# Cross-attention's value products in groups of 512 columns, each over both halves of the features

## What is computed

```python
def _cross_attention(h, mem_n, w_q, w_kv, w_o):
    B, S, _ = h.shape
    M = mem_n.shape[1]
    q = (h @ w_q).reshape(B, S, XA_HEADS, XA_HEAD_DIM)
    kv = (mem_n @ w_kv).reshape(B, M, 2, XA_HEADS, XA_HEAD_DIM)
    s = jnp.einsum('bshd,bmhd->bhsm', q, kv[:, :, 0]).astype(jnp.float32) * XA_HEAD_DIM ** -0.5
    p = jax.nn.softmax(s, axis=-1)
    o = jnp.einsum('bhsm,bmhd->bshd', p.astype(kv.dtype), kv[:, :, 1]).reshape(B, S, XA_HEADS * XA_HEAD_DIM)
    return o @ w_o
```

## Time and profile before

| | |
|---|---|
| Median of three runs | 1274.87 us (1273.26 to 1274.92) |
| The profiled execution, time | 1273.56 us |
| The profiled execution, span of the trace | 1271.6 us |
| TensorE (PE) busy | 1254.7 us, 99% of the span |
| Weight loads (PEld) busy | 1064.4 us, 84% |
| VectorE (DVE) busy | 823.1 us, 65% |
| ScalarE (ACT) busy | 666.0 us, 52% |
| GpSimd (POOL) busy | 208.7 us, 16% |

### The profile page before, as it was taken

One profiled execution on the slowest core, in us unless ns is written; L12 is line 12 of the kernel. 1 busy time (PEld: TensorE's weight loads), 2 busy tenths in 40 slices (PEclk: granted clock), 3 DMA queues, 4 the chain that ended last, 5 costly groups with the idle time before them and its releaser, 6 DMA issues.

```text
span 1271.6 us, 18501 instructions
## 1 busy us (share of the span) xinstructions
PE 1254.7 (99%) x6756; PEld 1064.4 (84%) x6756; DVE 823.1 (65%) x1185; ACT 666.0 (52%) x1119; POOL 208.7 (16%) x247
## 2 busy tenths in 40 slices
PE   8999999999999999999999999999999999999998
PEld 6888888899988888888888888888999798888886
DVE  5657777785566575555576568777857566755554
ACT  6454447664546464444564544565746465544442
POOL 1725541000001010000055246300000100100000
PEclk9999999999999999999999999999999999999999
DMA  9755453424525355555455554544255243655551
GB/s 346 270 188 179 168 194 146 166 100 170 196 100 182 106 229 198 198 183 182 167 185 192 198 198 165 192 156 160 74 182 204 112 150 133 235 191 177 181 181 62
DMA packets 32441, 222.34 MB, mean 175 GB/s; under 512 B 3584, under 2 KB 4096, under 8 KB 6784
## 3 DMA queue, kind: packets, MB, share of 16 engines
q1 hardware_dynamic: 30080, 209.28, 45.7%
q10 hardware_dynamic: 2304, 12.29, 2.6%
HBM read 219.46 MB, written 2.10 MB: 174 GB/s over the span
## 4 chain that ended last, share of the span: by engine, by line
PE 97%; DVE 1%; ACT 1%; issue 1%; DMA 0%; SPq 0%; POOLq 0%; ACTq 0%; POOL 0%; DVEq 0%
PE PS L1682 91%; PE PS L1769 2%; PE PS L1795 1%; PE PS L1991 1%; DVE w_lo L1161 1%; DMA raw<-in_weights 0%; ACT x_hi L717 0%; DVE x_lo L1164 0%; PE PS L1975 0%; PE PS L2273 0%; PE PS L2035 0%; PE PS L1922 0%; DVE h L1164 0%; PE PS L2042 0%; DVE work L1164 0%
## 5 line engine op out<-in xcount | busy, mean ns | idle before, releaser
L1161 DVE TENSOR_TENSOR w_lo<-raw,w_hi 128x1024 fp32r<-128x1024 f32 (+1 forms) x378 | 482.4, 1320 | 220.5 <-ACT w_hi L676 216.5
L676 ACT ACTIVATE w_hi<-raw 128x1024 fp32r<-128x1024 f32 x368 | 369.0, 1054 | 231.0 <-PE PS L1682 226.7
L1682 PE MATMUL PS<-w_hi,x_hi 128*128 128x512 f32 (+2 forms) x1136 | 438.3, 386 | 5.9 <-DVE x_lo L1164 3.0
L1682 PE MATMUL PS<-w_lo,x_hi 128*128 128x512 f32 (+2 forms) x1136 | 426.1, 375 | 0.0
L1682 PE MATMUL PS<-w_hi,x_lo 128*128 128x512 f32 (+2 forms) x1136 | 420.5, 376 | 0.0
L1682 PEld LDWEIGHTS PS<-w_hi,x_hi 128*128 128x128 f32 x1136 | 214.4, 189 | 48.9 <-issue 7.2
L1682 PEld LDWEIGHTS PS<-w_hi,x_lo 128*128 128x128 f32 x1136 | 214.3, 189 | 39.6
L1682 PEld LDWEIGHTS PS<-w_lo,x_hi 128*128 128x128 f32 x1136 | 214.8, 189 | 35.6 <-issue 0.5
L1682 PE MATMUL PS<-w_hi,hid_hi 128*128 128x512 f32 x336 | 131.5, 391 | 0.0
L1682 PE MATMUL PS<-w_lo,hid_hi 128*128 128x512 f32 x336 | 130.8, 389 | 0.0
L730 ACT ACTIVATE work<-PS,st 128x256 f32<-128x256 f32 x88 | 42.0, 478 | 155.5 <-PE PS L1682 153.9
(11 more groups left out here) (277 smaller groups left out, 1306.4 us busy)
## 6 DMA issues: line engine op xcount, KB each, us to landing
raw<-in_weights SPq DMA_DIRECT2D x194, 1024.0 KB, 4.7
pmat<-in_mats ACTq DMA_DIRECT2D x3, 1568.0 KB, 8.4
gain<-in_post ACTq DMA_DIRECT2D x8, 512.0 KB, 3.7
zone<-mem_scratch ACTq DMA_DIRECT2D x2, 1024.0 KB, 6.5
raw<-in_weights SPq DMA_DIRECT2D x3, 512.0 KB, 7.9
h<-in_x SPq DMA_DIRECT2D x2, 512.0 KB, 6.3
zone<-in_mem SPq DMA_DIRECT2D x1, 1024.0 KB, 9.7
mem_scratch<-zone ACTq DMA_DIRECT2D x1, 1024.0 KB, 5.6
```

Source lines behind the costliest of these rows:

```text
L676: a.activation(w_hi[s][:, c_], raw[s][:, c_], ACT.Copy).then_inc(sem[hi_done[s]], 1)
L1161: return v.tensor_tensor(o, x_, y_, op)
L1682: return t_.matmul(o, a_, b_, start=first, stop=last)
```

## The change

Per layer, the four value units become two pairs of units, (14, 15) and (16, 18). Each pair holds 512 value columns: its first unit carries the upper four feature tiles of them and its second unit the lower four. `values_half(pair, t, half)` is one part: four feature tiles, 12 matmuls of 512 columns, for token tile t. The two halves of one t accumulate into all of bank 1, which ScalarE then copies with `evac_values`. The semaphore `proj_half` tells of the end of t = 0 (so its count per layer goes from 5 to 7), `unit_done` that of t = 1. The host lays the weights out accordingly. There are still eight parts, but their order over the units is 14, 15, 14, 15, 16, 18, 16, 18 where it was 14, 14, 15, 15, 16, 16, 18, 18.

Because units 16 and 19 have one slot and one `unit_done`, `phi_unit(3)` (unit 19) moves behind part 7, which is the last use of unit 16; `times_values(1)` moves ahead of both, and the fold of the block rows behind part 8. VectorE's copy of the block rows moves behind `attention_out(1)`. On ScalarE the last evacuation moves from behind the tanh of the block rows to ahead of it, behind the split of unit 22.

```diff
-                proj_done=11, proj_half=5, s5_us=1, s5_u_dve=1, s5_t=1, s5_lb_act=1, s5_lb_dve=1, s5_k=1, s5_kd=1,
+                proj_done=11, proj_half=7, s5_us=1, s5_u_dve=1, s5_t=1, s5_lb_act=1, s5_lb_dve=1, s5_k=1, s5_kd=1,
...
+                def evac_values(pair, t):
+                    if t == 0:
+                        act.wait_ge(*E.at("proj_half", 5 + pair))
                     else:
-                        i = a.activation(xv[:, :, (q - 4) * UC:(q - 3) * UC],
-                                         v3(bank(KV_BANK[q]), "p (t n) -> p t n", t=TT), ACT.Copy)
-                    i.then_inc(sem["xkv_done"], 1)
+                        s, n, _ = mid(l, KV_UNITS[5 + 2 * pair])
+                        act.wait_ge(*E.at(unit_done[s], n + 1))
+                    act.wait_ge(*E.at("x_split", FILL[FI_MEM] + KT))
+                    a.activation(xv[:, t, pair * 512:(pair + 1) * 512], bank(1), ACT.Copy).then_inc(sem["xkv_done"], 1)
...
                 split_mid(22)
+                evac_values(1, 1)
                 act.wait_ge(*E.at("phi_x", 1))
                 a.activation(v3(hx2, "p (a n) -> p a n", n=NC_CMP), v3(hx2, "p (a n) -> p a n", n=NC_CMP),
                                  ACT.Tanh, scale=GELU_S).then_inc(sem["phi_th"], 1)
-                evac_kv(7)
                 split_mid(21)
...
                 split_mid(18)
                 attention_copy(1)
-                s, n, _ = mid(l, PHI_UNITS[3])
-                dve.wait_ge(*E.at(unit_done[s], n + 1))
-                v.tensor_copy(phi_rows, bank(0)).then_inc(sem["phi_h"], 1)
...
                 attention_out(1)
+                s, n, _ = mid(l, PHI_UNITS[3])
+                dve.wait_ge(*E.at(unit_done[s], n + 1))
+                v.tensor_copy(phi_rows, bank(0)).then_inc(sem["phi_h"], 1)
...
+                def values_half(pair, t, half):
+                    s, _, ns = mid(l, KV_UNITS[4 + 2 * pair + half])
+                    if half == 0:
+                        pe.wait_ge(*E.at("xkv_done", 4 + 2 * pair + t))
+                    pe.wait_ge(*E.at(split_done[s], ns + 1))
+                    for k in range(KT // 2):
+                        c_ = slice(k * 2 * UC, (k + 1) * 2 * UC)
+                        i = three([(x_tile(half * KT // 2 + k, t), (w_hi[s][:, c_], w_lo[s][:, c_]))], bank(1),
+                                  half == 0 and k == 0, half == 1 and k == KT // 2 - 1)
+                    if t == 1:
+                        i.then_inc(sem[unit_done[s]], 1)
+                    elif half == 1:
+                        i.then_inc(sem["proj_half"], 1)
...
-                kv_half(4, 0)
+                values_half(0, 0, 0)
                 probs_transposed(3)
-                kv_half(4, 1)
+                values_half(0, 0, 1)
                 times_values(3)
...
                 probs_transposed(1)
-                kv_half(6, 1)
-                phi_unit(3)
-                pe.wait_ge(*E.at("xkv_done", 7))
-                kv_half(7, 0)
+                values_half(1, 0, 1)
                 pe.wait_ge(*E.at("nsa_v", 1))
                 times_values(1)
+                values_half(1, 1, 0)
+                phi_unit(3)
+                values_half(1, 1, 1)
                 pe.wait_ge(*E.at("phi_h", 1))
...
                 i.then_inc(sem["phi_t"], 1)
-                kv_half(7, 1)
                 pe.wait_ge(*E.at("att_out", 3))
                 scores(2)
```

More of the change, by code:

```diff
@@ L943, in attention_t, with evac_keys @@
                     a.activation(probs_t[:, 0:1024], bank(5, 2), ACT.Copy).then_inc(sem["att_tc_act"], 1)
[L945 removed]
+                def evac_keys(q):
                     s, n, _ = mid(l, KV_UNITS[q])
                     act.wait_ge(*E.at(unit_done[s], n + 1))
[L948 to L955 removed]
+                    a.activation(zone[:, q * 512:(q + 1) * 512], bank(KV_BANK[q]), ACT.Copy).then_inc(sem["xkv_done"], 1)
+                def evac_values(pair, t):
+                    if t == 0:
+                        act.wait_ge(*E.at("proj_half", 5 + pair))
+                    else:
+                        s, n, _ = mid(l, KV_UNITS[5 + 2 * pair])
+                        act.wait_ge(*E.at(unit_done[s], n + 1))
+                    act.wait_ge(*E.at("x_split", FILL[FI_MEM] + KT))
+                    a.activation(xv[:, t, pair * 512:(pair + 1) * 512], bank(1), ACT.Copy).then_inc(sem["xkv_done"], 1)
                 def group_squares(groups, name, ready):
@@ L1003, in _ @@
                 split_mid(10)
-                evac_kv(0)
+                evac_keys(0)
                 attention_t(0)
-                evac_kv(1)
+                evac_keys(1)
                 split_mid(12)
@@ L1013, in _ @@
                 i.then_inc(sem["fox_nc"], 1)
-                evac_kv(2)
+                evac_keys(2)
                 act.wait_ge(*E.at("fox_tq", 1))
@@ L1017, in _ @@
                 split_mid(14)
-                evac_kv(3)
+                evac_keys(3)
                 attention(3)
@@ L1022, in _ @@
                 attention_t(3)
-                evac_kv(4)
+                evac_values(0, 0)
                 split_mid(16)
@@ L1026, in _ @@
                 a.activation(nsa_q[0:HD, :], bank(6, 2)[0:HD], ACT.Copy).then_inc(sem["nsa_tc_act"], 1)
-                evac_kv(5)
+                evac_values(0, 1)
                 attention(1)
@@ L1031, in _ @@
                 attention_t(1)
-                evac_kv(6)
+                evac_values(1, 0)
                 group_squares((0, 2), "att_out", 2)
@@ L1087, in xq_rows @@
                     if t == 0:
-                        act.wait_ge(*E.at("proj_half", 5))
+                        act.wait_ge(*E.at("proj_half", 7))
                     else:
@@ L2020, in kv_half @@
                             pe.wait_ge(*E.at("x_split", FILL[FI_MEM] + k + 1))
-                        if q < 4:
-                            c_ = slice(k * UC + part * P, k * UC + (part + 1) * P)
-                            i = three([((w_hi[s][:, c_], w_lo[s][:, c_]), (xh3[:, k], xl3[:, k]))],
-                                      o[:, part * S:(part + 1) * S], k == 0, k == KT - 1)
-                        else:
-                            c_ = slice(k * UC, (k + 1) * UC)
-                            i = three([(x_tile(k, part), (w_hi[s][:, c_], w_lo[s][:, c_]))],
-                                      o[:, part * UC:(part + 1) * UC], k == 0, k == KT - 1)
+                        c_ = slice(k * UC + part * P, k * UC + (part + 1) * P)
+                        i = three([((w_hi[s][:, c_], w_lo[s][:, c_]), (xh3[:, k], xl3[:, k]))],
+                                  o[:, part * S:(part + 1) * S], k == 0, k == KT - 1)
                     if part == 1:
                         i.then_inc(sem[unit_done[s]], 1)
+                def values_half(pair, t, half):
[11 more added lines that the diff above has]
+                        i.then_inc(sem["proj_half"], 1)
                 def fox_heads(at, b, name):
@@ L2150, in _ @@
                 i.then_inc(sem["nsa_t"], 1)
-                pe.wait_ge(*E.at("xkv_done", 5))
-                kv_half(5, 0)
+                values_half(0, 1, 0)
                 pe.wait_ge(*E.at("att_out", 2))
@@ L2383, in kv @@
         def kv(q):
-            put(tall(g["xa_w_kv"][l][:, q * UC:(q + 1) * UC]))
+            if q < 4:
+                put(tall(g["xa_w_kv"][l][:, q * UC:(q + 1) * UC]))
+            else:
+                at_, half = q // 2 * 2 * UC, q % 2
+                u = g["xa_w_kv"][l][:, at_:at_ + 2 * UC].reshape(KT, P, 2 * UC).transpose(1, 0, 2)
+                put(u[:, half * KT // 2:(half + 1) * KT // 2].reshape(P, UNIT))
         def phi(q):
```

11 lines of the change are left out of this document (2 added, 9 removed).

## The result

The changed kernel takes **1289.02 us** (median of 4 runs, 1288.55 to 1289.58) against 1274.07 for the kernel before: ratio 1.0117, 95% interval 1.0103 to 1.0132. It is 1.2% slower. The forecast was 1286.4 (1282.5 to 1290.0). The profiled execution has a span of 1286.7 us against 1271.6: 15.1 more, where 12.1 were forecast.

The account below looks back on a forecast made before the run. TensorE bounds the kernel (97% of the chain). Per layer, waits of 7.2 us less 1.1 saved; two layers +12.1 us, giving 1285.7 from the profile or 1287.0 from the median; the middle, 1286.4 us, range 1282.5 to 1290.

Parts of the forecast that it names:

- A: Before part 2, TensorE waits for VectorE's low half of unit 15: 2.0 us per layer.
- B: Before part 6, TensorE waits for VectorE's low half of unit 18: 1.5 us per layer.
- C: At the fold of the block rows, TensorE waits for VectorE's copy of them: 0.2 us per layer.
- D: Before the block's hidden product, TensorE waits for hidden rows, behind ScalarE's tanh and unit 22's split: 1.2 us per layer.
- E: Before out_rows(1, 0), TensorE waits for VectorE, late after splits of units 22 and 21: 2.3 us per layer.
- Savings: Eight value parts with 512-column matmuls, each 0.14 us shorter: 1.1 us less per layer.
- rival 4: The clock falls to the 1.2 GHz level at one wait of each layer: 2.0 us per layer, 1290.4 us; 6%.
- Rival 1: The tail is hidden (C to E don't occur), leaving A and B less savings: 4.8 us, 1279.7 us; 8%.
- Rivals 2 and 3: 2: early-wanted units are ready, only savings remain, 1272.7 us, 4%; 3: matmuls and waits cancel, about 1.3 more, 2%.

Follow-up runs that it names:

- e1_form: Kernel before, own order, each value part as 12 matmuls of 512 columns, not 24 of 256, lower four feature tiles left out; 1271.85 us, ratio 0.9987.
- e3_units: Changed kernel with unit 19 back behind part 6 (own semaphore), copy and fold where they were, tanh ahead of last evacuation; 1278.25 us, ratio 1.0036.
- e2_tail: e1_form with the change's places of unit 19, the fold, VectorE's copy and ScalarE's last evacuation, value units in old order; 1280.47 us, ratio 1.0051.
- e5_order: Changed kernel; ScalarE splits unit 21 before the tanh, unit 22 after; VectorE splits unit 22 behind mixer_lo and compressed scores; 1280.90 us, ratio 1.0068.
- e10_mixorder: e4_cover with units 14 and 15 in old form and order, and unit 21 split before unit 22 on ScalarE and VectorE; 1273.03 us, ratio 0.9995.
- e9_fill2: e7_fill plus three more 512-column matmuls, written to bank 5, between scores(2) and the wait for phi_hid; 1289.96 us, ratio 1.0126.
- e7_fill: Changed kernel plus nine 512-column matmuls ahead of out_rows(0, 0), which overwrites them; 1287.98 us, ratio 1.0115.
- e4_cover: e3_units with unit 19 ahead of part 6 and times_values(1) ahead of part 7; 1281.49 us, ratio 1.0055.
- e6_tanh: Changed kernel with ScalarE's tanh ahead of unit 22's split and the last evacuation behind that split; 1288.46 us, ratio 1.0104.

## Why the prediction was right, and where it was off

**Sign and mechanism: right.** TensorE bounds the kernel, and of the new 15.1 us, 12.4 are idle time of TensorE in the trace (6.2 a layer). e1_form shows that the form would have won 1.6 us over both layers; e3_units and e2_tail show that the two moves each cost more than that, and e5_order and e10_mixorder that the cost goes when the waits go. The measured 1289.02 us is inside the range but 2.6 above its middle, and the 2.9 us of the clock (below) are no term of the sum: the range, drawn for errors in the chains, held them by luck.

**The terms.** I compare when TensorE was ready with when it started; the trace's idle time is some 0.07 to 0.25 less, as it counts from the modelled end of the work before.
- *A*: forecast 2.0, measured 1.98 (315.52 less the end of `probs_transposed(3)`, 312.31 + 1.23).
- *B*: 1.5 and 1.46.
- *C*: 0.2 and 0.27. It shows as no pause, only as a fold at 349.64, 0.06 behind the end of the copy (348.89 + 0.69).
- *D*: 1.2 and 0.93. The chain was right: split 22 began 5.95 us after unit 19 (5.92 forecast). TensorE was the slower one: from unit 19 to the end of `scores(2)` took it 7.96 and not 7.71, half of it the fold (0.99 for 0.86).
- *E*: 2.3 and 2.4.
- *Savings*: 1.1 forecast, about 0.8 measured (0.84 in e1_form). A part took 3.01 us before and 2.90 in e1_form, means over both layers from its start to that of the next work, so 0.11 less and not 0.14. Its first step and its hand-over cost more than a step in between, but nearly the same in both forms: together 0.14 us over 24 and 12 even steps. What was off is the step inside a part, 0.230 us and not the 0.227 of the long stretch of the earlier trace rows, 0.03 over a part.

The five waits are 7.0 and less 0.8 that is 6.2; forecast 6.0. The stretches in which the clock stayed up while TensorE's order was the changed one, padded only inside the waits, agree: 57.34 in e9_fill2 and 57.40 in e7_fill, 6.13 and 6.19 over 51.21. The two misses, 0.3 less in D and 0.3 less in the savings, cancelled, which is luck.

**What was missing: the clock.** I gave rival 4 6%, at 2.0 us per layer. It came true in both layers of the profiled run, behind wait E, at 58.78 − 57.34 = 1.44 us. Twice 6.2 plus twice 1.4 is 15.2; the span grew by 15.1. The step that failed was the argument "the longest is 2.3 us, and TensorE works at 100% between them": between D and E it does so, on small products and on `out_rows(0, 0)`, and the clock fell all the same. The Trainium skill, TensorE: Matmul & The Clock Gate, "What's actually happening", says that TensorE's recent activity sets the level, which the fall at 364.30 behind pauses of 0.85 and 2.31 us agrees with; it also says that the chip judges this on a beat of its own, not the kernel's. That would fit e9_fill2, where two like layers came out 1.6 us apart, but no run here proves it.

**The rivals.** Rival 1 (hidden tail) is false for the changed kernel, by e2_tail; it is what e3_units and e5_order built on purpose, and they came out at +4.8 and +7.5 us by their medians against the kernel before on their chip (the profiled run of e5_order at +5.2), where it had 4.8. Rivals 2 and 3 fall with A and B measured.

**What stays open.** What decides whether the clock falls at a given place. Pauses of 0.8 us or more were there in most cases, not in all (none for e2_tail at 924.10 and e4_cover at 292.05, one of 0.24 us for e9_fill2 in layer 2), and e4_cover had the same 0.81 us with a fall and without. Behind waits A and B, pauses of 1.73 and 1.22 us, it never fell in any profile. So the length of a pause alone doesn't decide. And e7_fill and e9_fill2 do not gain by the median what their profiled layers gain; their other executions, which have no trace, had mean granted clocks of 0.993 to 0.996 against 0.998 in the profiled ones. That points at more falls, but the mean clock doesn't order all times: two runs of the changed kernel at 0.991 and 0.997 took 1289.22 and 1289.58 us.

## What to carry to other kernels

When TensorE is busy to 100%, an order that asks for an operand one step earlier costs the whole lateness of the chain that makes it, and shorter matmuls win little of it back (0.8 of 7.0 us a layer here): check, for each moved step, when its producer was released and not when it was needed before. Follow a moved step's side effects to the next load: here the late release of one raw slot put a split ahead of a small activation, and two waits came from it. Work put in front of a wait may only move it to the next one that hangs on the same chain, as in e4_cover. Price a pause not only by its length but also by a possible fall of the clock behind it, here 1.3 to 1.6 us for a low stretch of 3.41 us and 2.4 for the longer one of e6_tanh.

## What the runs showed of the hardware

- The granted clock fell to 0.50 in or behind pauses of 2.31 and even 0.81 us where small products stood near, and stayed there for 3.41 us, or at least 6.80 in e6_tanh. In the profiled kernel before, with pauses of up to 0.71 us behind the start, it did so only after the last matmul.
- It also fell in e2_tail and e4_cover without any pause, right behind a row of products with 1 to 128 columns in a stretch that is the same in all the kernels; that these products are the cause is not shown, as the other profiles have them with the clock up. Some runs of the kernel before may have such falls as well: of its 16 beside e5_order, those with a mean granted clock of 0.998 or more took 1272.6 to 1274.4 us, the two slowest (0.996 and 0.994) 1275.8 and 1278.0, and one more at 0.996 took 1274.4.
- The first step of a part is 0.31 to 0.34 us at 512 columns against 0.230 within it (e1_form), and 0.20 to 0.22 against 0.12 at 256 (before), so 0.09 to 0.10 more on average in either form. Twelve matmuls of 512 columns in place of 24 of 256 saved 0.105 us, not the 0.15 that steps of 0.227 and 0.12 promise.
